# A sparse-attention selection that searches raw float scores, and a gated unit and a swish spread over the last ten projection jobs

## The reference, cut to what matters

```
h = rms_norm(x);  (aq, ak, av, iq, ik, iw, za, uv, zb, glu, zc, gates) = split(h @ w_in)
score = einsum('bths,bth->bts', relu(einsum('bthd,bsd->bths', iq, ik)), iw)   # index heads
score = where(visible, score, -inf)
_, sel = top_k(score, 256)            # per query; chunks of 64 tokens are visible or not
logits = q . k[sel] - slope * |q_pos - sel|;  o_a = softmax(logits) @ v[sel]
o_b = u * (W_s layer_norm(v) + b)     # gated unit ("gmlp"): 128x128 mixing in chunks of 128
o_c = silu(layer_norm(causal_conv31(a * sigmoid(g))))        # conv module; its end is "swish"
x = x + (sum_b sigmoid(g_b) * ((o_b * silu(z_b)) @ w_b)) @ w_out
x = x + sigmoid(rms_norm(x) @ w_ple_gate) * (p @ w_ple);  final rms_norm
```

## Time and profile before

| | us |
|---|---|
| median of 3 runs (2899.11 to 2899.49) | 2899.15 |
| span of the profiled execution, first to last instruction | 2873.0 |
| TensorE busy in it | 2711.5 (94%) |
| VectorE busy | 2233.9 (78%) |
| ScalarE busy | 1496.9 (52%) |
| GpSimd busy | 1406.7 (49%) |
| mean granted TensorE clock | 0.979 of full |

### The profile page before, as it was taken

How to read it: one execution, slowest core, us unless ns; L and a number is a source line. 1 busy time by engine, 2 the same in 40 slices (tenths; PEclk the granted TensorE clock), 3 DMA queues, 4 the chain that set the end, 5 groups by cost and what they waited for, 6 DMA issues and landing times. The chain is left out here.

```text
span 2873.0 us, 40400 instructions
## 1 busy us (share of the span) xinstructions
PE 2711.5 (94%) x14029; PEld 2491.1 (87%) x14029; DVE 2233.9 (78%) x4177; ACT 1496.9 (52%) x2553; POOL 1406.7 (49%) x948
## 2 busy tenths in 40 slices
PE   6999999999999999999969778899989998999998
PEld 6999999999999999999868666777779997888886
DVE  6477969999999999999775578899976657555554
ACT  5377488776758776768412466777750002111111
POOL 1100289797897879697846463222163332111110
PEclk9999999999999999999989889999999999999999
DMA  4433323232332323232555633221165555122211
GB/s 166 122 125 119 108 87 122 88 121 97 122 123 91 103 79 111 83 124 74 173 191 176 182 95 81 75 59 52 40 221 177 164 189 178 48 72 72 64 56 38
DMA packets 271865, 320.95 MB, mean 112 GB/s; under 512 B 37041, under 2 KB 234545, under 8 KB 271021
## 3 DMA queue, kind: packets, MB, share of 16 engines
q1 hardware_dynamic: 171123, 190.55, 21.7%
q10 hardware_dynamic: 100538, 127.82, 12.8%
HBM read 196.42 MB, written 121.19 MB: 111 GB/s over the span
## 5 line engine op out<-in xcount | busy, mean ns | idle before, releaser
L1638 PE MATMUL psum<-hT_hi,j_whi 128*128 128x416 f32 x2440 | 876.5, 359 | 6.5 <-POOL j_wlo L1447 3.8
L1638 PE MATMUL psum<-hT_hi,j_wlo 128*128 128x416 f32 x2440 | 862.0, 353 | 0.0
L1638 PE MATMUL psum<-hT_lo,j_whi 128*128 128x416 f32 x2440 | 861.8, 353 | 0.0
L1253 POOL TENSOR_TENSOR v_y<-v_y,v_product 128x422 f32<-128x422 f32 x540 | 694.5, 1324 | 68.4 <-ACT v_product L1235 68.3
L1638 PEld LDWEIGHTS psum<-hT_hi,j_whi 128*128 128x128 f32 x2440 | 463.7, 190 | 17.0 <-issue 9.2
L1638 PEld LDWEIGHTS psum<-hT_lo,j_whi 128*128 128x128 f32 x2440 | 464.7, 190 | 9.8 <-issue 1.8
L1638 PEld LDWEIGHTS psum<-hT_hi,j_wlo 128*128 128x128 f32 x2440 | 463.2, 190 | 5.9
L1235 ACT ACTIVATE v_product<-v_x,v_taps 128x422 f32<-128x422 f32 x600 | 361.2, 643 | 147.7 <-POOL v_y L1253 118.1
L433 DVE TENSOR_SCALAR_CACHE_REDUCE s_high<-s_key,s_cand 128x512 int16<-128x512 f32 (+13 forms) x240 | 354.5, 1477 | 8.4
L1447 POOL TENSOR_TENSOR j_wlo<-j_w,j_whi 128x1024 fp32r<-128x1024 f32 x61 | 153.8, 2521 | 272.5 <-ACT j_whi L1482 272.4
L1500 ACT ACTIVATE j_out<-psum 128x416 f32<-128x416 f32 x285 | 143.9, 506 | 255.9 <-PE psum L1638 238.6
(11 more groups left out here) (306 smaller groups left out, 5235.7 us busy)
## 6 DMA issues: line engine op xcount, KB each, us to landing
T_dram<-j_out ACTq DMA_DIRECT2D x59, 624.0 KB, 2.9
j_w<-in_w_in ACTq DMA_DIRECT2D x59, 512.0 KB, 3.9
m_gate<-T_dram SPq DMA_DIRECT2D x60, 416.0 KB, 3.5
T_dram<-j_out ACTq DMA_DIRECT2D x59, 416.0 KB, 2.4
m_oraw<-B_dram SPq DMA_DIRECT2D x15, 832.0 KB, 5.3
M_dram<-m_merged ACTq DMA_DIRECT2D x5, 1664.0 KB, 7.8
n_x<-in_x_prompt SPq DMA_DIRECT2D x16, 512.0 KB, 5.0
f_mraw<-M_dram SPq DMA_DIRECT2D x16, 512.0 KB, 4.6
```

The source lines that it names most:

```text
L1253: pool.tensor_tensor(y[k % 2][:], y[k % 2][:], product[n % RING][:], ALU.add).then_inc(added, 1)
L1638: last = pe.matmul(bank, w[p][:, k, :], h[:, k, t0:t0 + SPAN], start=(k == 0 and q == 0), stop=(k == KD - 1 and q == 2))
```

## The change

Five things are changed.
- The search. VectorE compares the raw float scores with a candidate whose bit pattern it builds (`bits`, an int32 read as a float), over 32 bits for a whole tile and 16 for a completion. The passes that turned the scores into ordered integers and split them (`prepare`, L446 to L451; L459, L460) go, and so do L462, L467, L470 and L472. Scores that are not visible get a large negative number in a corner of 64x64 (`taken_up`). The distances come from one table. The update of the candidate after each count is an XOR of two tensors.
- ScalarE's search: 15 steps a tile instead of 16, each with four activations instead of three.
- `ACT_DUE` and `FINISHED` are computed by `select_times` from a price per key and per bit; they end the selection at 302.4 + 854.7 us instead of 302.4 + 1075.
- The convolution takes 43 jobs instead of 47 (14.4 taps a job on average, 13.2 before). The gated unit starts at (50, 4) instead of (55, 2) and gives each pair of tiles 20 slices instead of 8; swish gives each of its steps 28 slices instead of 20.
- `rest_of_units` is called once more, ahead of two of the gated unit's loads. Tiles 0 to 3 lose the padding to 512 keys.

```diff
@@ -196,8 +186,8 @@
-CONV_FROM, CONV_JOBS = 9, 47
-GMLP_FROM = (55, 2)
+CONV_FROM, CONV_JOBS = 9, 43
+GMLP_FROM = (50, 4)
...
-    return PAST + DEC if t == DT else P * max(4, t + 1)
+    return PAST + DEC if t == DT else P * (t + 1)
...
-ACT_DUE = [30, 99, 229, 379, 541, 706, 846, 968]
 LOADED = [(9, 0), (4, 1), (12, 2), (5, 1), (13, 0), (6, 1), (14, 2), (7, 1), (15, 0), (DT, 1), (11, 2), (2, 1), (10, 0), (3, 1), (8, 2)]
-FINISHED = [(4, 89), (9, 152), (5, 219), (12, 294), (6, 368), (13, 449), (7, 530), (14, 615), (DT, 697), (15, 784), (2, 837), (11, 907), (3, 960), (10, 1025), (8, 1075)]
+def select_times():
+    us, due, done = 0.0, [], []
+    def spend(t, columns, steps):
+        nonlocal us
+        us += 0.00104 * columns * keys_of(t) + 0.8 * steps
+    def offer(t):
+        spend(t, 1, 3)
+        due.append(us + 10 + 0.03 * us)
+    def finish(t, bits):
+        spend(t, bits + 6.8, bits + 2)
+        done.append((t, us))
+    offer(ACT_TILES[0])
+    finish(DVE_TILES[0], 32)
+    for x, t in enumerate(ACT_TILES[1:]):
+        offer(t)
+        finish(ACT_TILES[x], 16)
+        if x + 1 < len(DVE_TILES):
+            finish(DVE_TILES[x + 1], 32)
+    finish(ACT_TILES[-1], 16)
+    return due, done
+ACT_DUE, FINISHED = select_times()
...
-            self.act, self.steps, self.turn, self.bit = act, Steps(act, act_steps), 0, 15
+            self.act, self.steps, self.turn, self.bit = act, Steps(act, act_steps), 0, 14
...
-            return keys_of(ACT_TILES[self.turn]) * 0.00084 + 0.95
+            return keys_of(ACT_TILES[self.turn]) * 0.00084 + 1.25
...
-            do(act.activation(a_junk[:, 0:n], high[HIGH_HALF[t]][:, 0:n], ACT.Sign, bias=bias, accum_out=a_cnt[:]))
-            do(act.activation(a_sign[:], a_cnt[:], ACT.Sign, bias=a_full[n][:]))
+            do(act.activation(a_junk[:, 0:n], tops, ACT.Sign, scale=a_sign[:, p:p + 1], bias=level, accum_out=a_cnt[:]))
+            do(act.activation(a_turn[:], a_cnt[:], ACT.Sign, bias=a_least[:, p:p + 1]))
             if b:
-                do(act.activation(a_bias[:], a_sign[:], ACT.Identity, scale=-(2.0 ** (b - 1)), bias=bias))
+                do(act.activation(a_bits[:], a_turn[:], ACT.Identity, scale=2.0 ** (b + 15), bias=value))
+                self.steps.did(act.activation(a_value[:], a_turn[:], ACT.Identity, scale=2.0 ** (b + 15), bias=value))
                 self.bit -= 1
             else:
-                act.activation(a_found[self.turn % 2][:], a_sign[:], ACT.Identity, scale=-0.5, bias=bias).then_inc(found, 1)
-                self.turn, self.bit = self.turn + 1, 15
+                act.activation(a_found[p][:], a_turn[:], ACT.Identity, scale=2.0 ** 15, bias=value).then_inc(found, 1)
+                self.turn, self.bit = self.turn + 1, 14
...
-        def search(src, junk, first):
-            do(vec.tensor_scalar(cand[:], c.zero[:], float(first + 2 ** 15), None, ALU.add))
-            for b in reversed(range(16)):
-                do(vec.tensor_scalar(junk, src, cand[:], 0.0, ALU.is_ge, ALU.add, accum_out=cnt[:]))
-                do(vec.tensor_scalar(g[:], cnt[:], float(TOPK), float(2 ** b), ALU.is_ge, ALU.mult))
-                do(vec.tensor_scalar(cand[:], g[:], cand[:], -(2.0 ** (b - 1)) if b else -1.0, ALU.add, ALU.add))
...
-            do(vec.tensor_scalar(above, H[:, 0:n], threshold, 65536.0, off, ALU.mult))
-            do(vec.scalar_tensor_tensor(out=K, in0=low, scalar=1.0, in1=above, op0=ALU.add, op1=ALU.add))
...
-            do(vec.tensor_scalar(e, e, need[:], None, ALU.is_gt))
-            for x, (a, w) in enumerate(pieces(n)):
-                do(vec.tensor_scalar(K[:, a:a + w], iota[:, 0:w], -1.0, q_from[:, x, t:t + 1], ALU.mult, ALU.add))
...
+        def search(t, top):
+            K, n = key[slot[t]], keys_of(t)
+            for b in reversed(range(top + 1)):
+                do(vec.tensor_scalar(tie[:, 0:n], K[:, 0:n], bits[:].bitcast(F32), 0.0, ALU.is_ge, ALU.add, accum_out=cnt[:]))
+                do(vec.tensor_scalar(flip[:], cnt[:], float(TOPK), 2.0 ** b if b < 31 else -1.0, ALU.is_lt, ALU.mult))
+                if b:
+                    do(vec.scalar_tensor_tensor(out=bits[:], in0=flip[:], scalar=1 << (b - 1), in1=bits[:],
+                                                op0=ALU.bitwise_xor, op1=ALU.bitwise_xor))
+                else:
+                    do(vec.tensor_tensor(bits[:], flip[:], bits[:], ALU.bitwise_xor))
+        def taken_up(t):
+            n, k = keys_of(t), slot[t]
+            vec.wait_ge(full[k], turn[t] * 16 + 16)
+            if t != DT:
+                do(vec.memset(key[k][0:CHUNK, n - CHUNK:n], HIDDEN))
+        def finish(t):
+            n, at = keys_of(t), SEQ - P - (PAST if t == DT else P * t)
+            K, e, least = key[slot[t]][:, 0:n], tie[:, 0:n], bits[:].bitcast(F32)
+            do(vec.tensor_scalar(e, K, least, 0.0, ALU.is_gt, ALU.add, accum_out=cnt[:]))
+            do(vec.tensor_scalar(rank[:], cnt[:], -TOPK - 0.5, TIE, ALU.add, ALU.mult))
+            do(vec.tensor_scalar(e, K, least, TIE, ALU.is_equal, ALU.mult))
+            do(vec.tensor_tensor_scan(e, e, e, rank[:], ALU.add, ALU.min))
+            do(vec.scalar_tensor_tensor(out=e, in0=K, scalar=least, in1=e, op0=ALU.subtract, op1=ALU.is_lt))
+            vec.scalar_tensor_tensor(out=K, in0=e, scalar=MASKED, in1=distance[:, at:at + n], op0=ALU.mult, op1=ALU.max
+                                     ).then_inc(done[slot[t]], 1)
 
         def whole(t):
-            prepare(t)
-            n, H = keys_of(t), high[HIGH_HALF[t]]
-            search(H[:, 0:n], wide_junk[:, 0:n] if 2 * n > SEQ else H[:, SEQ - n:SEQ], 0)
-            finish(t, cand[:], ALU.subtract)
+            taken_up(t)
+            do(vec.memset(bits[:], 0))
+            search(t, 31)
+            finish(t)
 
         def offer(x):
-            prepare(ACT_TILES[x])
+            t, p = ACT_TILES[x], x % 2
+            n, room = keys_of(t), keys_of(t) - 2 * TOPK + 1
+            taken_up(t)
+            do(vec.tensor_scalar(tie[:, 0:n], key[slot[t]][:, 0:n], 0.0, 0.0, ALU.is_ge, ALU.add, accum_out=cnt[:]))
+            do(vec.tensor_scalar(up[:], cnt[:], float(TOPK), 2.0, ALU.is_ge, ALU.mult))
+            steps.did(vec.tensor_scalar(a_sign[:, p:p + 1], up[:], 2.0 ** LIFT, -(2.0 ** LIFT), ALU.mult, ALU.add))
+            steps.did(vec.tensor_scalar(a_least[:, p:p + 1], up[:], float(room), -float(room), ALU.mult, ALU.add))
+            steps.did(vec.tensor_scalar(a_mask[p][:].bitcast(I16)[:, 1:2], up[:], -(2.0 ** 14), None, ALU.mult))
+            do(vec.tensor_scalar(a_mask[p][:].bitcast(U16)[:, 0:1], up[:], 0.5, 2.0 ** 15 - 1, ALU.mult, ALU.add))
-            finish(ACT_TILES[x], a_found[x % 2][:], ALU.add)
+            do(vec.tensor_scalar(bits[:], a_found[p][:], -float(LIFT << 23), None, ALU.add))
+            do(vec.tensor_tensor(bits[:], bits[:], a_mask[p][:], ALU.bitwise_xor))
+            search(t, 15)
+            finish(t)
...
+        do(vec.scalar_tensor_tensor(out=distance[:], in0=distance[:], scalar=-1.0, in1=distance[:], op0=ALU.mult, op1=ALU.max))
...
-    TURN_AT, MIX_AT = (0, 4), (2, 6)
-    first_span = c.gmlp_span = GMLP_FROM[0] * len(SPANS) + GMLP_FROM[1]
-    c.gmlp_spans = LAG + len(PAIRS)
+    STEP, TURN_AT, MIX_AT = 20, (0, 10), (5, 15)
+    first_slice = (GMLP_FROM[0] * len(SPANS) + GMLP_FROM[1]) * KD
+    c.after_gated_unit = first_slice + (LAG + len(PAIRS)) * STEP
...
+        rest_of_units(job_us(*GMLP_FROM))
...
-        d = j * len(SPANS) + b - first_span
+        d, k = divmod((j * len(SPANS) + b) * KD + k - first_slice, STEP)
...
-    STEP, SQUARES, SPREAD = 20, 15, 27
-    first_slice = (c.gmlp_span + c.gmlp_spans) * KD
+    STEP, SQUARES, SPREAD = 28, 15, 27
+    first_slice = c.after_gated_unit
```

More of the change, by code:

```diff
@@ L152, in stage_constants @@
 def stage_constants(c):
[L154 to L155 removed]
+    scale_made = c.sem("c_scale_made")
     def gpsimd(pool):
@@ L160, in gpsimd @@
             pool.wait_ge(scale_made, h + 1)
[L161 to L169, removed]
     c.wait_for_scale = lambda eng: eng.wait_ge(scale_made, HEADS)
-    return Programs(gpsimd=gpsimd, vector=vector)
+    return Programs(gpsimd=gpsimd)
 LEFT = CONV - 1
@@ L315, in stage_select @@
     nc, sb = c.nc, Sbuf(c.nc, c.after_convolve)
[L316 to L319, removed]
-    a_cnt, a_sign, a_bias = (sb(f"s_a{n}", [P, 1]) for n in ("cnt", "sign", "bias"))
-    a_found = [sb(f"s_afound{k}", [P, 1]) for k in range(2)]
-    a_sizes = sorted({keys_of(t) for t in ACT_TILES})
-    a_start, a_full = sb("s_astart", [P, 1]), {n: sb(f"s_afull{n}", [P, 1]) for n in a_sizes}
-    q_from = sb("s_qfrom", [P, SEQ // PIECE, TILES])
-    lim_from, q_tail = sb("s_limfrom", [P, TILES]), sb("s_qtail", [P, TILES])
-    a_junk = sb("s_ajunk", [P, SEQ], U8)
-    wide_junk = sb("s_widejunk", [P, keys_of(DT)], U16)
+    key = [sb(f"s_key{k}", [P, SEQ]) for k in range(KEYS)]
+    distance = sb("s_distance", [P, SEQ], I16)
+    tie = sb("s_tie", [P, SEQ], BF16)
+    a_junk = sb("s_ajunk", [P, SEQ], U8)
```

(27 more changed lines are left out.)

75 lines of the change are left out of this document (25 added, 50 removed).

## The result

The changed kernel takes 2974.6 us (median of four runs, 2968.5 to 2977.9) against 2899.3 for the kernel before, a ratio of 1.0259, 95% interval 1.0225 to 1.0293: 75 us slower, where 2964 had been forecast.

What follows compares the result with a forecast made beforehand. TensorE's trunk sets the pace until 1400 us, then gated unit and swish, held back by the selection, cost 50 us; 2899 - 42 - 24 = 2833, plus 131 of stalls, gave 2964, range 2875 to 3015.

Steps and rivals of the forecast that it cites:

- The base of 2833: Whole kernel before stalls: 2899 less 42 us for the tail and 24 us for the middle.
- the 26.1 us that I had put around the span: Gap between the profiled execution's 2873.0 us and the runs' median, carried unchanged.
- What the change can win: Tail, 1400 to 1620 us: 42 of 50 lost us won by spreading gated unit and swish; bounds 20 to 50.
- the middle's own losses: TensorE, 300 to 1400 us: 16 us of waits and about 8 of clock, taken off as 24; bounds 0 to 24.
- The bits update: VectorE's L451, two tensors: stands until half a running GpSimd tap (0.53 us, share 0.8) ends; mean near 0.58 us.
- w: Wait per bit in VectorE's search, taken as 0.42 us, bounds 0 to 0.6; a hundredth is worth 3.2 us.
- the 894 named: VectorE's selection without the wait w, forecast to fall from 1107 us to 894.
- Where the wait surfaces: Offers and unit loads: ScalarE slips 162 us, 85 at offers; less 31 of allowance and catch-up, 131 reach TensorE.
- my four late units: Conv units 13, 15 and 17 late by 16, 7 and 13 us, unit 18 by 39; loads behind stores on SyncE.
- A: VectorE's update doesn't wait (w up to 0.1); only unit 18's stall is left: 2855 to 2885 us, chance 0.20.
- C: ScalarE and GpSimd have no room in jobs 18 to 34; adds up to 40 us: 2980 to 3040, chance 0.08.
- B: VectorE's update waits half as often (w 0.1 to 0.25): 2885 to 2909 us, chance 0.14.

Runs made afterwards that it cites:

- the 2807 us kernel: Changed kernel with the one-input update and SyncE's finish times written out, each completion waiting for ScalarE's threshold: 2807.1 us, ratio to the kernel before 0.9695.
- the two kernels without late units: Changed kernel with 1.15 us instead of 0.8 in select_times, 2896.2 us; changed kernel with the finish times of the 2807 us kernel, 2860.3 us.
- the last plan: Changed kernel, two-input update kept, with finish times and ScalarE's due times both written for its wait: 2894.7 us, ratio to the kernel before 0.9983.
- the run: Changed kernel with only the candidate's update (L451 and L454) written as one tensor and a scalar by pointer: 2931.9 us, ratio to the kernel before 1.0122.
- the fourth corner: Changed kernel, two-input update kept, with the finish times of the 2807 us kernel: 2860.3 us, ratio to the kernel before 0.9874.

## Why the prediction came out right, and where it did not

**The sum.** +65 us forecast, +75 measured. It came near by luck as well, by terms that were not all right. The base of 2833 carried the 26.1 us that I had put around the span. Only 2 us lie there; without the 26 the base is 2807, and the kernel in which no unit is late takes 2807.1. So the stalls cost 167 us, not 131, and the 26 us covered most of the difference. A slip besides: 49, 5 and 8 us make 62 for unit 18, not 60, and the recorded total of 162 holds 41 for it, not the 39 named.

**What the change can win.** Right in kind and size, where nothing is late: 47 us against 42 (2853.9 - 2807.1). The changed kernel didn't win it, it lost 73 by the spread. The further 24 us for the middle's own losses were about right: the 2807 us kernel leaves 4 us of idle there, at a clock of 1.00, where 16 and 0.99 were, and with the old spread it spans 21 us less than the kernel before (2852.1 against 2873.0).

**The bits update.** Right: 0.543 us against the 0.58 named, w = 0.38 against 0.42, the two-input row carried over as it stood. Its direct price, 43 to 53 us, was shown in both kernels and under both plans. As a picture, half a running tap is wrong all the same. Most waits are set by the number of keys and lie between nothing and 0.95 us (last section), and a few are far longer. The few are what raises the mean where GpSimd hardly idles: w is 0.53 us in the two kernels without late units (690 and 695 ns less 0.16) and 0.59 in the last plan, but without the updates over 2.6 us it is 0.34 in the changed kernel and 0.37 to 0.42 in those three. That half a tap gave 0.42 for 0.38 is in part luck. The Trainium skill's exclusive lock ("SBUF — State Buffer", section "Who interferes with whom") is borne out: the same update took 214 ns beside the same taps as soon as one operand came by pointer.

**The end of the selection.** 1350 forecast, 1360.5 measured, but of other parts. From 293 us on VectorE waits 135.6 us for thresholds and 129 in the updates, which leaves some 802 for the work. My prices give 861 for the fifteen tiles (the 894 named isn't reached by them), so the work was priced some 58 us too high and the updates 19, and the waits for thresholds, for which the 1350 left some 48, came to 88 more.

**Where the wait surfaces: the step that failed.** The forecast had 85 us at offers and 77 at unit loads. Measured were 14.3 us at one offer and 186 us of GpSimd's waits at units. I took a unit's loads to be needed at ScalarE's copy of the taps. They are needed before that: `CONV_TIMES` puts GpSimd's L1248 half a unit, 5.4 spans or 24 us, ahead of the first tap, and in GpSimd's straight program everything behind it stops. Unit 17 shows it, L1248 at 1276.26 and the copy at 1295.99. With the need 24 us too late in my chain, stalls of 24 us and less were invisible, at w = 0 above all: there it gave 43 us of slip and 2855 us, and the run gave 138 us of waits and 2932. With 24 us more each, my four late units come to 171 us, near the 186. And since each unit's stall sets ScalarE back, the offers, which I had late, came in time: where no unit is late, in the fourth corner, they cost 83.1 us, as the 85 of the forecast. Two errors on one chain offset each other: the wait was charged with 109 us (2964 - 2855), measured 43 to 53, and the plan with the order on SyncE with 22 (2855 - 2833), measured 114 to 125.

**The plan.** I wrote that it prices a bit too low. The heavier fault was not the bit price: `select_times` adds up VectorE's work alone and has no term for a completion that waits for ScalarE's threshold. The finish times that have this term, 12 to 63 us later from tile 9 on, won 114 and 125 us with the bit price left as it was. My own chain had the number (tile 9's threshold at 374, its end at 426; the plan has it done at 302 + 106) and did not set it against the plan's list. Nor did I ask what slack the old spread had given to such an error: there it costs 5 us.

**The rivals.** A, no wait, is refuted as a description of this kernel, and its price (2855 to 2885) as a description of that case: without the wait it is still 1.2% slower than before. C, no room, is refuted for the new search by 1096 of 1100 us busy at 14.4 taps a job, once nothing is late. B asked for a w of half the size; it was not.

## What to carry to other kernels

A small instruction of two SBUF tensors in a chain on VectorE, beside a GpSimd that hardly rests, can cost a wait each time; give it the second operand by pointer. When programs of in-order engines are laid out from a table of expected times, the table must hold every wait of the thing it predicts, here ScalarE's search as well as VectorE's bits: a load that stands behind a store that comes later than planned (the last one here at 1360 us, planned for 1157) stops engines that have nothing to do with either. An error in such a table can lie hidden in slack, so a change that takes slack away has to be priced together with it: here a spread worth 47 us cost 73. When looking for the moment by which a load is needed, take the first instruction in any engine's program that waits for it, not the one where the work starts. And when a profiled execution is faster than the median, ask whether the difference lies outside the span before carrying it over.

## What the runs showed of the hardware

The usual wait is not half of a tap on average, by chance; the two engines fall into step. With GpSimd's taps back to back at 1.064 us, VectorE's bit at 1792 keys, which would take about 2.5 us (3.18 less the 0.67 by which the update is longer than 0.16), came every 3.18 to 3.19 us, three whole taps, with the update at 0.83 us each time. It is so for the other tiles of the changed kernel, beside taps that follow each other without a gap. At 384 keys a bit comes every 1.06 us and the update takes 0.17. From 512 to 1408 keys a bit comes every 2.1 us, whatever its size, and the update takes 1.1 us at 512 keys, 0.83 at 768, 0.57 at 1024, 0.31 at 1280 and 0.17 at 1408. So such a chain has its round lengthened to a whole number of the other engine's instructions, and the same small instruction costs nothing at one size and almost a whole tap at another. In the changed kernel and three of its two-input variants 479 of the 486 bits in such stretches came within 0.15 us of one, two or three taps.

The exceptions are rare and dear. In the changed kernel, four of its two-input variants and the kernel before with two inputs, 19 updates stood for 3.7 to 24.7 us while GpSimd ran from 3 up to 21 further instructions past them. Each of the 19 ended together with a GpSimd instruction behind which GpSimd paused. The two-input form with the old spread had none, and the one-input update never took over 0.22 us. What makes an update miss its turn is not shown.
